# Normed rows written by VectorE into the PSUM banks of the expert sums

## The chip, the cores and the metric

The kernel runs on one core of one Trainium2 chip. The metric is the device time of one execution in microseconds. Everything is float32.

## The reference

Two transformer blocks over 256 tokens of width 1024 run one after the other. What matters here is the first block, which has two layers. Each layer is a mixer (a convolution module in layer 0, a differential attention in layer 1), a layer norm, a mixture of experts, and a second layer norm:

```
for l in range(DEPTH):
    mix = conformer_conv(...) if l < N_A else diff_attention(...)
    x = layer_norm(ALPHA * x + mix, ln_mix_g[l], ln_mix_b[l])
    ffn = grouped_moe(x, router_w, router_bias, moe_w_gate[l], moe_w_up[l], moe_w_down[l])
    x = layer_norm(ALPHA * x + ffn, ln_ffn_g[l], ln_ffn_b[l])
```

`layer_norm` is `(x - mean) * rsqrt(var + 1e-5) * g + b` over the 1024 columns. `grouped_moe` picks two of 16 experts for each token by a sigmoid router, and adds `(silu(x @ wg) * (x @ wu)) @ wd` of the chosen experts with weights that sum to one. The sum over the experts is added to `ALPHA * x`, so the normed rows x are both the input of the experts and a term of their sum.

## The kernel before

**Stages.** One program writes a queue for each engine (TensorE as `pe`, ScalarE as `act`, VectorE as `dve`, GpSimd as `pool`, SyncE as `sp`), stage after stage in the list `ORDER`. Most stages have no barrier between them; engines meet through semaphores. Tokens are two tiles of 128 rows, t = 1 and 2. PSUM has 8 banks of 128 x 512. Banks 0 to 3 are taken in turn by numbered jobs: `take_bank(j)` waits until the bank was read out, `job_done` counts finished jobs, and `job_ready(eng, j)` lets an engine wait for job j. Banks 4 to 7 hold running sums: `layer_sum(t)` is the pair of banks 4, 5 for t = 1 and 6, 7 for t = 2.

**Around the change, layer 0.** In `conformer`, banks 4 to 6 hold the sums for a norm over the channels. Then `project_and_turn` multiplies the activated convolution output with `pw2`: four parts of eight 128x512 products (L623), each part a 512-column half of a tile; the first part waits chunk by chunk for ScalarE's SiLU (`act_ready`, L1033). VectorE adds the residual, takes mean and variance and writes the normalized, unscaled rows to `xhat[t - 1]` (L602, `centred_scaled`). TensorE transposes them (L531) and ScalarE and VectorE copy the transposes out with gain and bias to `xT` (L556, L558). Only then does VectorE run `natural_rows`: for each tile xhat times gain into `x_nat` (L610), then `x_nat` plus bias into `x_nat` (L611). `natural_rows` is called three times: by `mix_norm` (k = 0), by `ffn_norm` of layer 0 (k = 1) and by `mix_norm1` (k = 2).

**The router** (`route`, once for each layer). TensorE multiplies `xT` with the router's weights (L1211), ScalarE copies the parts (L1152), TensorE sums them (L1217), ScalarE takes the sigmoid (L1154). VectorE, behind `natural_rows` in its queue, ranks the experts in some 17 small dependent operations (L1167 to L1193), and the last of them raises `won_ready`. Meanwhile TensorE puts x into the sums as products of x with the identity (L1224), two halves for each tile, with `start=True`, so that the experts' products, all with `start=False`, add to it. Behind them in TensorE's queue stand jobs J + 2 and J + 3 (L255, narrow products that count each expert's tokens), which wait for `won_ready`. VectorE turns job J + 2 into seats (L1202, then L1427). ScalarE copies `x_nat` in another order of columns to `by_row` (L1158), once for each tile, and raises `rows_ready`.

**The experts** (`experts`). TensorE waits for `rows_ready` and for the seats and gathers the tokens of the first pair of experts (`gather`, L255, 32 records of 128x128), then multiplies with the gate and up weights of each expert (L1565), transposes, multiplies with the down weights (L1598) and scatters into banks 4 to 7 (L1608). The expert weights, 48 units of 2 MB for each layer, are streamed by SyncE's queue (L421) in order. Each unit waits until the last product on the slot that it overwrites: in each layer the unit issued after pair 0's first gate and up products (`GU0`) is the first of the pair's slots to come free. Two of the extra slots lie in `x_nat` and `norm_rows`; they wait for `rows_ready` and for job J + 2.

Of the kernel before, what the change touches and what calls it, by code (L numbers as in the profile page):

```python
# [25 lines left out]
ALU = mybir.AluOpType  # L26
# [5 lines left out]
KC = D // P  # L32
# [30 lines left out]
BANKS = 4  # L63
# [47 lines left out]
def first_jobs():  # L111
    at, out = 0, {}
    for name, n in JOBS:
        out[name] = at
        at += n
    return out
# [41 lines left out]
def program(nc, a, out):  # L158
# [3 lines left out]
    def sb(name, *shape):  # L162
        return ctx.enter_context(nc.sbuf_tensor(name, list(shape), F32))

    def sem(name):
        return ctx.enter_context(nc.semaphore(name))

    FJ = first_jobs()
# [5 lines left out]
    x_nat = sb("x_nat", P, 3, D)  # L174
    xT = sb("xT", P, KC, L)
    norm_rows = sb("norm_rows", P, 2, 2, D)
    vec = sb("vec", P, len(VEC_ROWS) * P)
    ident = sb("ident", P, P)
    ones = sb("ones", P, P)
# [22 lines left out]
    psum = ctx.enter_context(nc.psum_tensor("psum", [P, 8, 512], F32))  # L202
# [14 lines left out]
    dve_step, act_step = Chain(nc.vector, sem("dve_step")), Chain(nc.scalar, sem("act_step"))  # L217
# [18 lines left out]
    def bank(j):  # L236
        return psum[:, j % BANKS, :]

    def take_bank(j):

        if j >= BANKS:
            nc.tensor.wait_ge(bank_free[j % BANKS], j // BANKS)

    def job_ready(eng, j):
        eng.wait_ge(job_done, j + 1)
# [6 lines left out]
    def products(dst, pairs):  # L252

        for n, (lhsT, rhs) in enumerate(pairs):
            last = nc.tensor.matmul(dst, lhsT, rhs, start=(n == 0), stop=(n == len(pairs) - 1))  # L255
        return last
# [15 lines left out]
    unit_at = {}  # L272
# [83 lines left out]
    def slot(u):  # L356
        return arena[:, 6690:6690 + 4096] if slots[u] == RING else ring[:, slots[u], :]
# [8 lines left out]
    def slot_k(u, n=512):  # L366

        return slot(u).rearrange("p (k n) -> p k n", n=n)

    def unit_ready(u):  # L370
        nc.tensor.wait_ge(slot_loaded[slots[u]], landed[u])
# [214 lines left out]
    xhat = carve(13300, D), carve(5664, D)  # L586
# [11 lines left out]
    def centred_scaled(t, root, normed, src, dst):  # L598
# [2 lines left out]
        reciprocal_of(nc.vector, var, root)  # L601
        nc.vector.tensor_scalar(dst, src, mean, var, ALU.subtract, ALU.mult).then_inc(normed, 1)  # L602

    def natural_rows(k, normed, xhat=xhat):

        dve = nc.vector
        dve.wait_ge(norm_loaded[k % 2], 32 * (k // 2 + 1))
        dve.wait_ge(normed, 2)
        for t in (1, 2):
            dve_step(dve.tensor_tensor(x_nat[:, t, :], xhat[t - 1], norm_rows[:, k % 2, 0, :], ALU.mult))  # L610
            dve.tensor_tensor(x_nat[:, t, :], x_nat[:, t, :], norm_rows[:, k % 2, 1, :], ALU.add).then_inc(normed, 1)  # L611

    def project_and_turn(first, u0, lhs, normed, ready=None):

        pe = nc.tensor

        def part(j, half, t):
            unit_ready(u0 + half)
            take_bank(j)
            for k in range(KC):  # L620
                if ready is not None and half == 0:
                    ready(k, t)
                last = pe.matmul(bank(j), lhs(k, t), slot_k(u0 + half)[:, k, :], start=(k == 0), stop=(k == KC - 1))  # L623
            last.then_inc(job_done, 1)

        def turn(j, t):
            transposes_pe(j, (t,), lambda t: xhat[t - 1], lambda t: pe.wait_ge(normed, t))

        part(first, 0, 1)
        part(first + 1, 1, 1)  # L630
        part(first + 2, 0, 2)
        turn(first + 3, 1)
        part(first + 5, 1, 2)
        turn(first + 6, 2)
# [237 lines left out]
    mean_summed, conv_normed, act_ready = sem("mean_summed"), sem("conv_normed"), sem("conv_activated")  # L872
    normed = [sem(f"normed{k}") for k in range(4)]
# [3 lines left out]
    def conformer():  # L877
# [3 lines left out]
        def _(pe):  # L881
# [67 lines left out]
            for c in (6, 7):  # L949
# [5 lines left out]
            products(bank(FJ["iota"])[:, 0:P], [(ones[:, :], upto[:, :])]).then_inc(job_done, 1)  # L955
            take_bank(FJ["relb"])
            products(bank(FJ["relb"])[0:HEADS, 0:3 * P], [(rel_w[:, :], buckets)]).then_inc(job_done, 1)
            project_and_turn(FJ["mix0"], unit_at["pw2"], lambda k, t: conv[:, k, (t - 1) * P:t * P], normed[0],
                             ready=lambda k, t: pe.wait_ge(act_ready, KC * (t - 1) + k + 1))

# [162 lines left out]
    by_row = carve(4640, 2, KC, P)  # L1123
# [11 lines left out]
    def layer_sum(t):  # L1135

        return psum[:, BANKS + 2 * t - 2:BANKS + 2 * t, :].rearrange("p b n -> p (b n)")
# [7 lines left out]
    def route(layer):  # L1145
# [3 lines left out]
        @block.scalar  # L1149
        def _(act):  # L1150
            job_ready(act, J)
            act.activation(parts, bank(J)[:, 0:SEQ], ACT.Copy).then_inc(bank_free[J % BANKS], 1)  # L1152
            job_ready(act, J + 1)
            act.activation(aff[:, :, :], bank(J + 1)[:, 0:2 * EXPERTS].rearrange("p (t e) -> p t e", t=2),  # L1154
                           ACT.Sigmoid).then_inc(aff_ready, 1)
            for t in range(2):
                act.wait_ge(normed[2 * layer], 3 + t)
                act_step(act.activation(by_row[:, t, :, :], x_nat[:, t + 1, :].rearrange("p (f k) -> p k f", k=KC),  # L1158
                                        ACT.Copy))
            act.nop().then_inc(rows_ready, 1)  # L1160

# [44 lines left out]
        @block.tensor  # L1206
        def _(pe):
            all_read_out(pe, J)
            for r in range(2):
                for g in range(CONV_GROUPS):  # L1210
                    last = pe.matmul(bank(J)[32 * g:32 * g + 32, 0:SEQ], router_w[:, 4 * r + g, :],  # L1211
                                     xT[:, 4 * r + g, META:L], start=(r == 0), stop=(r == 1))
            last.then_inc(job_done, 1)
            take_bank(J + 1)
            pe.wait_ge(bank_free[J % BANKS], J // BANKS + 1)
            for t in range(2):
                last = pe.matmul(bank(J + 1)[:, t * EXPERTS:t * EXPERTS + EXPERTS], parts[:, t * P:t * P + P],  # L1217
                                 quad_diag[:, 0:EXPERTS], start=True, stop=True)
            last.then_inc(job_done, 1)

            for t in (1, 2):
                pe.wait_ge(normed[2 * layer], 2 + t)
                for half in range(2):
                    pe.matmul(psum[:, BANKS + 2 * t - 2 + half, :], ident[:, :], x_nat[:, t, half * 512:half * 512 + 512],  # L1224
                              start=True, stop=False, skip_group_check=True)
            take_bank(J + 2)
            take_bank(J + 3)
            pe.wait_ge(won_ready, layer + 1)
            n = EXPERTS
            products(bank(J + 2)[:, 0:n], [(upto[:, :], beats[:, 0, :])])  # L1230
            products(bank(J + 2)[:, n:2 * n], [(ones[:, :], beats[:, 0, :]), (upto[:, :], beats[:, 1, :])]).then_inc(
                job_done, 1)
            products(bank(J + 3)[:, 0:n], [(ones[:, :], beats[:, 0, :]), (ones[:, :], beats[:, 1, :])]).then_inc(job_done, 1)
# [1819 lines left out]
```

## Time and profile before

| | |
|---|---|
| median of 3 runs | 1397.87 us (1395.96 to 1400.76) |
| the profiled execution's own time | 1401.46 us |
| its span | 1399.7 us |
| TensorE matmul busy | 1306.0 us, 93% |
| VectorE busy | 383.9 us, 27% |
| ScalarE busy | 262.6 us, 19% |
| bytes moved | 321.68 MB, mean 230 GB/s |
| chain that ended last | PE 87%, DMA 5%, DVE 5% |

### The profile page before, as it was taken

Reading aid. Unit: us, or ns where it says so; the run is one execution under the profiler, and the core shown is the slowest. Engines: PE = TensorE matmul, PEld = TensorE weight load, DVE = VectorE, ACT = ScalarE, POOL = GpSimd, SP = SyncE. Lnnn points to the kernel's source line nnn. Section 1 sums busy time; section 2 is a strip of 40 time slices with the busy share of each in tenths; the row PEclk is TensorE's granted clock in tenths of the full one; section 3 lists DMA queues with packets and bytes.
Section 4 is the critical chain, followed back from the end, with each engine's and each line's share of the span. In section 5 each row is a group of like instructions: output and inputs, shape, how many; then the busy total and the mean of one; then the engine's idle time right before and its main releaser. Section 6 shows DMA issues by size and latency. Waiting matters only on the chain.

```text
span 1399.7 us, 14987 instructions
## 1 busy us (share of the span) xinstructions
PE 1306.0 (93%) x6166; PEld 815.9 (58%) x6166; DVE 383.9 (27%) x849; ACT 262.6 (19%) x579; POOL 36.0 (3%) x62
## 2 busy tenths in 40 slices
PE   7989899999989998999999799998998979999997
PEld 6754444333437864433433388765775867888743
DVE  0014522111142454312211403455223123222101
ACT  1013311000111343200100321412435012000000
POOL 3110000000000000000000000000000000000000
PEclk9999999999999998999999899899999998999999
DMA  9970899999992063999999923231230162444320
GB/s 307 309 249 2 324 407 428 425 423 429 415 380 86 1 240 147 418 426 424 427 427 427 393 109 121 67 110 43 84 120 1 35 193 73 153 147 161 141 90 30
DMA packets 95087, 321.68 MB, mean 230 GB/s; under 512 B 10099, under 2 KB 47511, under 8 KB 80167
## 3 DMA queue, kind: packets, MB, share of 16 engines
q1 hardware_dynamic: 84368, 301.04, 55.5%
q10 hardware_dynamic: 8662, 12.27, 2.8%
q0 software_dynamic: 1984, 7.34, 1.3%
q8 instruction: 53, 0.87, 0.3%
q14 instruction: 20, 0.16, 0.0%
HBM read 316.30 MB, written 4.34 MB: 229 GB/s over the span
## 4 chain that ended last, share of the span: by engine, by line
PE 87%; DMA 5%; DVE 5%; issue 1%; ACT 1%; DVEq 0%; ACTq 0%; SPq 0%; POOLq 0%
PE psum L255 35%; PE psum L1565 14%; PE psum L1598 7%; PE psum L741 6%; PE psum L2917 5%; DMA ring<-in_moe_w_up 5%; PE psum L1608 4%; PE psum L623 2%; PE psum L909 2%; PE psum L1802 2%; PE psum L531 1%; PE psum L1767 1%; DMA ring<-in_a_w_pw 1%; PE psum L2577 1%; PE psum L1224 1%
## 5 line engine op out<-in xcount | busy, mean ns | idle before, releaser
L255 PE MATMUL psum<-xT,ring 128*128 128x256 f32 (+2 forms) x1792 | 409.7, 390 | 4.6 <-DMA ring<-in_a_w_pw 3.7
L255 PEld LDWEIGHTS psum<-xT,ring 128*128 128x128 f32 x1792 | 344.9, 194 | 65.4 <-issue 10.4
L1565 PE MATMUL psum<-ring,arena 128*64 128x512 f32 x672 | 186.0, 604 | 12.1 <-DMA ring<-in_moe_w_up 6.6
L1565 PEld LDWEIGHTS psum<-ring,arena 128*64 128x64 f32 x672 | 59.8, 139 | 103.1 <-issue 102.8
L1446 DVE TENSOR_TENSOR arena<-psum,arena 64x512 f32<-64x512 f32 x32 | 34.2, 1070 | 215.7 <-ACT arena L1509 215.7
L1598 PE MATMUL psum<-ring,arena 128*64 128x512 f32 x384 | 85.0, 595 | 1.3 <-ACT arena L1526 1.3
L2917 PE MATMUL psum<-ring,arena 128*128 128x512 f32 x176 | 75.7, 592 | 0.0
L1565 PE MATMUL psum<-arena 128*64 128x512 f32 x208 | 70.6, 592 | 0.0
L1509 ACT ACTIVATE arena<-psum 64x512 f32<-64x512 f32 x32 | 18.9, 592 | 269.8 <-PE psum L1565 269.8
L1608 PE MATMUL psum<-arena 128*128 128x512 f32 x128 | 59.5, 605 | 0.0
L2917 PEld LDWEIGHTS psum<-ring,arena 128*128 128x128 f32 x176 | 33.4, 190 | 41.7 <-issue 41.6
L1598 PEld LDWEIGHTS psum<-ring,arena 128*64 128x64 f32 x384 | 27.4, 137 | 51.7 <-issue 51.5
L741 PE MATMUL psum<-arena,ring 128*128 128x258 f32 x256 | 55.8, 381 | 0.0
L255 PE MATMUL psum<-arena 128*128 128x128 f32 (+3 forms) x372 | 52.8, 291 | 1.9 <-issue 1.9
L741 PEld LDWEIGHTS psum<-arena,ring 128*128 128x128 f32 x256 | 48.6, 190 | 7.0
L255 PEld LDWEIGHTS psum<-arena 128*128 128x128 f32 (+1 forms) x372 | 43.5, 182 | 10.0 <-issue 9.2
L531 PE MATMUL psum<-ident,arena 128*128 128x128 f32 (+1 forms) x120 | 19.3, 324 | 29.6 <-DVE arena L2069 19.1
L1608 PEld LDWEIGHTS psum<-arena 128*128 128x128 f32 x128 | 22.8, 189 | 35.0 <-issue 35.0
L1470 DVE COPY arena<-psum 128x512 f32<-128x512 f32 x16 | 11.1, 692 | 98.7 <-PE psum L1598 98.7
L531 PEld LDWEIGHTS psum<-ident,arena 128*128 128x128 f32 (+1 forms) x120 | 16.9, 180 | 34.4 <-DVE arena L2069 20.2
L2944 ACT ACTIVATE arena<-arena 128x256 f32<-128x256 f32 x22 | 9.2, 416 | 143.1 <-DVE arena L2961 143.1
L909 PE MATMUL psum<-arena 128*32 128x256 f32 x512 | 31.0, 396 | 4.7 <-issue 4.7
(343 smaller groups left out, 1310.2 us busy)
## 6 DMA issues: line engine op xcount, KB each, us to landing
ring<-in_moe_w_down SPq DMA_DIRECT2D x24, 2048.0 KB, 24.9
ring<-in_moe_w_up SPq DMA_DIRECT2D x22, 2048.0 KB, 20.7
ring<-in_moe_w_gate SPq DMA_DIRECT2D x20, 2048.0 KB, 22.7
ring<-in_w_in SPq DMA_DIRECT2D x11, 2048.0 KB, 22.3
ring<-in_w_up SPq DMA_DIRECT2D x22, 1024.0 KB, 7.7
arena<-in_moe_w_gate SPq DMA_DIRECT2D x6, 2048.0 KB, 26.3
ring<-in_w_down SPq DMA_DIRECT2D x5, 2048.0 KB, 7.8
ring<-in_a_w_pw SPq DMA_DIRECT2D x8, 1024.0 KB, 10.9
```

The lines of the kernel that those rows point to most:

```text
L255: last = nc.tensor.matmul(dst, lhsT, rhs, start=(n == 0), stop=(n == len(pairs) - 1))
L531: last = nc.tensor.transpose(bank(j)[:, c * P:c * P + n], src(t)[0:n, at:at + P], ident[0:n, 0:n])
L623: last = pe.matmul(bank(j), lhs(k, t), slot_k(u0 + half)[:, k, :], start=(k == 0), stop=(k == KC - 1))
L741: last = nc.tensor.matmul(bank(first + c)[:, NEED:L], slot_k(part_units[half])[:, k, (c % 4) * P:(c % 4) * P + P], src[:, k, NEED:L], star ...
L909: last = pe.matmul(bank(j)[32 * g:32 * g + 32, 0:SEQ], blocks[:, c % BLOCK_BUFS, q, g, :], shifted[:, c % REP_BUFS, g, 4 * q:4 * q + SEQ], ...
L1446: dve.tensor_tensor(hid_both[part, :].rearrange("s (k f) -> s k f", f=P), by_row(bank(j)[part, :]), by_row(silu_g[part, 0, :]), ALU.mult). ...
L1509: act.activation(silu_g[UP_IN[side], 0, :], bank(j)[GATE_IN[side], :], ACT.Silu).then_inc(silu_ready, 1)
L1565: last = pe.matmul(bank(j)[part, :], tokens[:, k, side * SEATS:side * SEATS + SEATS], weights(u + n, k), start=(k == 0), stop=(k == KC - 1))
L1598: last = pe.matmul(bank(j)[part, :], hidT_both[:, k, side * SEATS:side * SEATS + SEATS], weights(u + side, k, D)[:, half * 512:half * 512 ...
L1608: last = pe.matmul(psum[:, BANKS + 2 * t + half, :], gatedT[:, p % 4, t * P:t * P + P], y_pair[:, half * 512:half * 512 + 512], start=Fals ...
L1802: last = pe.matmul(psum[:, BANKS + 2 * (t - 1) + half, :], oT[:, h, TILE_AT[t]:TILE_AT[t] + P], slot_k(unit_at["w_o"] + half)[:, h, :], st ...
L2917: last = pe.matmul(psum[:, BANKS + 2 * t + half, :], fT[:, c, t * P:t * P + P], slot_k(u, D)[:, c % 4, half * 512:half * 512 + 512], start ...
```

## The change

In `natural_rows` the second operation of each tile writes into `layer_sum(t)`, the two PSUM banks, where k is even; for k = 1 it still writes `x_nat`. The first operation works in place in `xhat`, so VectorE first waits for the job that transposed that tile (`turned_job`). ScalarE's copy to `by_row` reads `layer_sum` in place of `x_nat`. The four products with the identity are gone in both layers. PSUM keeps a flag for each element that says whether a product adds or overwrites, and only products set it; so in layer 0, ahead of `project_and_turn`, four products of one row are put in, one for each of banks 4 to 7, whose result is later overwritten. They wait for the weights of `pw2` and for the first SiLU.

```diff
+    def turned_job(k, t):
+
+        return FJ["mix0"] + (4, 7)[t - 1] if k == 0 else FJ["ffn0_xT" if k == 1 else "mix1"] + 2 * t - 1
+
     def natural_rows(k, normed, xhat=xhat):
 
         dve = nc.vector
         dve.wait_ge(norm_loaded[k % 2], 32 * (k // 2 + 1))
         dve.wait_ge(normed, 2)
         for t in (1, 2):
-            dve_step(dve.tensor_tensor(x_nat[:, t, :], xhat[t - 1], norm_rows[:, k % 2, 0, :], ALU.mult))
-            dve.tensor_tensor(x_nat[:, t, :], x_nat[:, t, :], norm_rows[:, k % 2, 1, :], ALU.add).then_inc(normed, 1)
+            job_ready(dve, turned_job(k, t))
+            dst = x_nat[:, t, :] if k % 2 else layer_sum(t)
+            dve_step(dve.tensor_tensor(xhat[t - 1], xhat[t - 1], norm_rows[:, k % 2, 0, :], ALU.mult))
+            dve.tensor_tensor(dst, xhat[t - 1], norm_rows[:, k % 2, 1, :], ALU.add).then_inc(normed, 1)
...
+            unit_ready(unit_at["pw2"])
+            pe.wait_ge(act_ready, 1)
+            for b in range(BANKS, 2 * BANKS):
+                pe.matmul(psum[:, b, :], ones[0:1, :], slot_k(unit_at["pw2"])[0:1, 0, :], start=True, stop=True)
             project_and_turn(FJ["mix0"], unit_at["pw2"], lambda k, t: conv[:, k, (t - 1) * P:t * P], normed[0],
...
-                act_step(act.activation(by_row[:, t, :, :], x_nat[:, t + 1, :].rearrange("p (f k) -> p k f", k=KC),
+                act_step(act.activation(by_row[:, t, :, :], layer_sum(t + 1).rearrange("p (f k) -> p k f", k=KC),
                                         ACT.Copy))
...
-            for t in (1, 2):
-                pe.wait_ge(normed[2 * layer], 2 + t)
-                for half in range(2):
-                    pe.matmul(psum[:, BANKS + 2 * t - 2 + half, :], ident[:, :], x_nat[:, t, half * 512:half * 512 + 512],
-                              start=True, stop=False, skip_group_check=True)
```

## Rows read from the trace of the kernel before

**Rows 1.** Chain that ended last, layer 0: start us, us, what.

```profile
119.06 23.78 PE psum L623 x48
160.00 4.85 PE psum L1224 x8
```

**Rows 2.** Timeline before and in the `pw2` projection: start us, us, engine, line.

```profile
115.66 0.81 PE L255 MATMUL psum<-arena,rel_w 32*8 32x384 f32 x2
118.42 3.86 ACT L1033 ACTIVATE arena<-arena,vec 128x128 f32<-128x128 f32 x8
120.90 0.34 PEld L623 LDWEIGHTS psum<-ring,arena 128*128 128x128 f32 x1 [0.52 <-issue]
121.75 0.34 PEld L623 LDWEIGHTS psum<-ring,arena 128*128 128x128 f32 x1 [0.52 <-ACT arena L1033]
137.53 5.31 PE L623 MATMUL psum<-ring,arena 128*128 128x512 f32 x12
```

**Rows 3.** Timeline of the router, layer 0.

```profile
158.99 1.01 PE L1217 MATMUL psum<-quad_diag,arena 128*128 128x16 f32 x4 [0.59 <-ACT arena L1152]
159.77 1.23 DVE L611 TENSOR_TENSOR x_nat<-x_nat,norm_rows 128x1024 f32<-128x1024 f32 x1
159.84 5.01 PE L1224 MATMUL psum<-x_nat,ident 128*128 128x512 f32 x8
160.04 0.20 ACT L1154 ACTIVATE arena<-psum 128x32 f32<-128x32 f32 x1 [1.19 <-PE psum L1217]
160.13 4.16 ACT L1158 ACTIVATE arena<-x_nat 128x1024 f32<-128x1024 f32 x2
164.30 0.19 DVE L1193 SCALAR_TENSOR_TENSOR arena<-arena 128x32 f32<-128x32 f32 x1
164.69 0.31 PE L255 MATMUL psum<-arena,upto 128*128 128x16 f32 x2
165.56 0.19 DVE L1202 TENSOR_TENSOR arena<-arena,psum 128x32 f32<-128x32 f32 x1 [0.19 <-PE psum L255]
166.84 3.81 PE L255 MATMUL psum<-arena 128*128 128x128 f32 x32 [0.94 <-issue]
```

**Rows 4.** Timeline of the router, layer 1.

```profile
557.66 5.77 PE L1224 MATMUL psum<-x_nat,ident 128*128 128x512 f32 x8
562.13 0.19 DVE L1193 SCALAR_TENSOR_TENSOR arena<-arena 128x32 f32<-128x32 f32 x1
563.28 0.29 PE L255 MATMUL psum<-arena,upto 128*128 128x16 f32 x2
```

**Rows 5.** Group of instructions by line: count, then busy us and mean ns.

```profile
L602 DVE TENSOR_SCALAR arena<-psum,small 128x1024 f32<-128x1024 f32 x4 | 5.4, 1344 | 0.1
```

**Rows 6.** Stretches: from:to us, length, PE busy (records), PEclk, DMA share, GB/s.

```profile
124.00:125.00 1.00, 1.00 (x2) 0.51 0.00 0
155.00:156.00 1.00, 0.00 (x0) 0.85 1.03 442
162.00:163.00 1.00, 1.00 (x3) 0.73 0.84 352
343.00:344.00 1.00, 1.00 (x6) 0.78 1.04 442
882.00:883.00 1.00, 1.00 (x10) 0.87 1.08 414
```

**Rows 7.** Timeline of TensorE at a wait for weights and at narrow products.

```profile
340.44 5.98 PE L1565 MATMUL psum<-ring,arena 128*64 128x512 f32 x20 [2.69 <-DMA ring<-in_moe_w_up]
879.19 4.75 PE L255 MATMUL psum<-w_dt,xT 128*16 128x16 f32 x48
```

**Rows 8.** Timeline of SyncE's queue, layer 0.

```profile
177.71 0.33 SPq L421 DMA_DIRECT2D ring<-in_moe_w_up  x1
```

**Rows 9.** Stretches: from:to us, length, PEclk, DMA share, GB/s.

```profile
178.00:180.00 2.00, 1.00 0.81 193
578.50:579.00 0.50, 1.00 1.06 377
```

## The prediction

> **What bounds the kernel now.** I read the chain of waits first. It runs through TensorE for 87% of the span, and both places that the change touches lie on it: the `pw2` projection as one unbroken piece of 23.78 us, and the identity products with 4.85 us in layer 0 [rows 1]. A piece on the chain is only what its engine did while the next thing was awaited, so I then read the timeline around each to see what else ended at the same moment.
>
> In layer 0's router the identity products are issued at 159.84 and job J + 2 behind them starts at 164.69. VectorE's last ranking operation ends at 164.30 + 0.19 = 164.49, and a start 0.20 us behind it is what the semaphore alone would give. So VectorE's chain and the identity products end together, and taking the products away frees nothing there [rows 3]. In layer 1 VectorE ends at 562.32 and J + 2 starts at 563.28; with the same 0.20 us it could start at 562.52, so the products hold it up by about 0.75 us [rows 4]. Behind that come the seats, which ride on J + 2 (read by VectorE at 165.56), and then the gather at 166.84. ScalarE's copies to `by_row` end at 164.29, 2.5 us before the gather needs them [rows 3].
>
> VectorE's chain itself starts where `natural_rows` ends, at 161.00, not at the sigmoid, which ended at 160.24 [rows 3]. So the two writes into PSUM are on the path.
>
> Then the views by stretches, for TensorE's clock and the DMA. The clock is at its lower level (1.2 GHz, 0.50) from about 155.7 to 162.5 us: TensorE had been mostly idle ahead of 155.7, and it rose again while the identity products ran [rows 3, 6]. It is full when the gather starts. The DMA runs at some 426 GB/s through most of each expert stage. The PE waits 2.69 us for weights late in layer 0's stage [rows 7], so the end of the stage is set by the queue of weight transfers, and that by the last place where the queue ran dry. In layer 0 this is at 178 to 180 us, where it moved 193 GB/s; the unit that fills it again is issued at 177.71, on the heels of pair 0's first products [rows 8, 9]. In layer 1 the same place shows a mere dent, 377 GB/s for half a microsecond [rows 9]: 0.06 us lost. So whatever makes pair 0 later makes the stage later in layer 0 one for one, and in layer 1 too after a margin that I take as 0.2 us; making it earlier gains at most the hole, (1 - 193/426) x 2 = 1.1 us in layer 0, and nothing in layer 1.
>
> **The change part by part.**
>
> *Four products of one row, added.* Each is two records. A record of 512 columns takes 5.31/12 = 0.43 us at the full clock, and 0.85 us at the lower one (starts at 120.90 and 121.75) [rows 2]. That the operand has one row should not shorten it: two records of 384 columns with 32 rows took 0.81 us [rows 2], no less than their columns ask for. They wait for the first SiLU, as the projection does. The SiLUs come at 3.86/8 = 0.48 us [rows 2] and the projection needs two records for each, so TensorE, not ScalarE, sets the pace from 119.06 on, and nothing hides the four. The clock was low from there to about 124.98, 5.9 us after the products began [rows 1, 6]. If the added products count as work for the clock like the ones that they displace, the low stretch holds them in place of the projection's first records, which then run at the full clock: the cost is 8 x 0.43 = 3.4 us. If they don't, it is 8 x 0.85 = 6.8 us. I take 3.4, since streaming columns is what the displaced ones do too. This delays everything behind, the weight transfers also: those of layer 0 wait for the projection's jobs.
>
> The Trainium skill, "PSUM — Partial Sum Buffer", under "The four PSUM rules", says that VectorE's writes leave the add-or-overwrite bits alone, and that a seed other than zero should go in through TensorE by an identity product. That speaks against this change and is the reason for the added products; without it the sum would be 3.4 us smaller. No row of this trace shows the bits.
>
> *`natural_rows`.* The same four operations. The multiplies stay as they are. No row shows VectorE writing PSUM. Nearest is one reading PSUM, 1.344 us for 128x1024 [rows 5], against 1.23 for the add into SBUF [rows 3]: between 0 and 0.12 us more for each of two tiles. I take 0.06, so 0.1 us on each layer's path. The added waits are for transposes that `scaled_out` in the same queue has already waited for: nothing. For k = 1 VectorE works beside TensorE's attention projections: nothing.
>
> *The copy to `by_row` from PSUM.* 4.16/2 = 2.08 us now; it would have to take over 3.3 us each (2.08 + 2.5/2) to matter, and it may be faster, which gains nothing since the seats come last [rows 3]. Zero.
>
> *The identity products, gone.* 0 in layer 0 and -0.75 in layer 1, from above. But they were also what TensorE did while it waited. Without them it is idle from the end of L1217 at 160.0 until J + 2 at about 164.6, and the clock, low at 160, has nothing to bring it back. J + 2 and J + 3 are too narrow for that: 48 records of 16 columns kept TensorE "busy" for 4.75 us, and the clock fell at the end of them [rows 6, 7]. So J + 2 starts at the lower level. L1217 there shows 0.25 us for such a record, against some 0.14 for the six of J + 2 now (164.69 to about 165.5): 6 x 0.1, with less for the weight load's share, makes 0.5 us [rows 3].
>
> The gather is then the first dense work. How long does the low clock last behind such a start? After 119.06 it was 5.9 us; after 340.44 about 3.0 [rows 1, 6, 7]. I take the middle, 4.5 us. Gather and first expert products are paced by TensorE at half speed in it, so half is lost: 2.25 us, from 1.5 to 3.0. I choose this over no loss because the clock was already low when the idle stretch began.
>
> The Trainium skill, "TensorE: Matmul & The Clock Gate", under "The HAM clock gate", has it that the lower clock is the default and activity releases it. By that rule the gather pays; by a clock that came back by itself it would not, and the sum would be 4.5 us smaller. The rows agree with the rule.
>
> *The sum.* Layer 0: 3.4 + 0.1 + 0.5 + 2.25 = 6.25 us, all of it passed on by the dry weight queue. Layer 1: 0.1 + 0.5 + 2.25 - 0.75 - 0.2 = 1.9. Together 8.15 us on the profiled execution's own 1401.46, so 1409.6. That execution was 3.6 us above the median of the runs shown; on 1397.87 the same sum gives 1406.0, which I take.
>
> **The rivals.**
>
> *The clock is back for the gather.* If the small products or the neighbouring work bring it back, 3.4 + 0.1 + 0.5 remain in layer 0 and nothing in layer 1: 4.0 us, 1401.9. For it: layer 0's low stretch was over 2.7 us into the identity products [rows 3, 6]. Against it: 2.5 us of that came behind continuous dense work that is gone.
>
> *The added products don't count for the clock.* Then 3.4 more: 1409.4. Nothing in the trace has so few rows.
>
> *The weight queue hides the gather.* If queued transfers reach further than I read, the slower start of pair 0 is absorbed by the PE's later wait of 2.69 us, and 3.5 to 4 us remain: 1401.6. The hole at 178 us speaks against it [rows 9].
>
> *The identity products were the bound (the other side).* If the chain is taken at its word, 4.85 us go in layer 0 and about as much in layer 1 (5.77 us busy), less 3.4 added: about -7 us, 1391. It decides only if VectorE's ranking would end that much sooner, or the copies to `by_row` were what the gather waited for and became quick from PSUM. VectorE's own end at 164.49 speaks against it [rows 3].
>
> **How the numbers follow.** About 0.3% (4.2 us) is what a measurement of this kernel tells from no change. The forecast gets 0.50, with its own range of 1402.5 to 1409.5 (loss at the gather 1.5 to 3.0 in each layer, PSUM writes 0 to 0.25, and the spread of the runs). The clock rival has 0.22, the uncounted products 0.12, the queue 0.08, the other side 0.08. Slower by over 0.3%: nearly all of the forecast and of the uncounted products, and a third of the two at 1401.6 to 1401.9, so 0.70. Faster 0.08, the rest 0.22. For 8 in 10 the range reaches from the two cases near 1401.7, less the spread of the runs, to the uncounted products: 1398 to 1411.
>
> **What would show it.** L623 unbroken as before, behind eight records of one row that take about 5.9 us at the low clock, with the projection's end 3.4 us later against its first SiLU. `natural_rows` at about 1.22 and 1.23 to 1.35 us. An idle TensorE between L1217 and J + 2, PEclk 0.50 through J + 2 and into the gather, and the gather at about 6 to 7 us in place of 3.81. The unit issued behind pair 0's first products later against the start of the gather, and a deeper hole in the DMA behind it, in layer 1 a first one. The prediction is wrong if the gather still takes 3.8 us, if the added products take the place of idle time, or if layer 1's expert stage ends no later against its attention.

## The result, and the profile after

The changed kernel takes 1405.03 us (median of 6 runs, 1404.13 to 1410.46), the kernel before 1398.51 beside it (6 runs, 1395.96 to 1400.76). The ratio is 1.0056, with an interval of 1.0035 to 1.0076: 7.8 us slower, between 4.9 and 10.6. The prediction was 1406.0, or 8.15 us slower than the 1397.87 that it started from. The profiled execution of the changed kernel took 1404.13 us, its span 1402.4, against 1401.46 and 1399.7 before. These two single executions are only 2.7 us apart: the one of after is the fastest of its six. So the runs carry the size of the effect, and the profiles its place.

The engines' busy time, from the head of the page of after:

```profile
span 1402.4 us, 14972 instructions
PE 1302.7 (93%) x6158; PEld 818.7 (58%) x6158; DVE 384.0 (27%) x849; ACT 258.3 (18%) x579; POOL 35.9 (3%) x62
```

TensorE's time fell by 3.3 us and ScalarE's by 4.3, and the kernel became slower. The totals cannot tell why, so I read the two places in their order. First the projection, in TensorE's timeline of after (start us, us, engine, line, out<-in, count, and in brackets the idle time before it and what ended it):

```profile
112.41 0.81 PE L255 MATMUL psum<-arena,rel_w 32*8 32x384 f32 x2
115.81 5.56 PE L967 MATMUL psum<-ring,ones 1*128 1x512 f32 x8 [2.59 <-ACT arena L1043]
121.30 9.87 PE L629 MATMUL psum<-ring,arena 128*128 128x512 f32 x19
```

and in its stretches (from:to us, length, PE busy and records, PEclk, DMA share, GB/s); the last three belong to the router and to layer 1:

```profile
117.00:118.00 1.00, 1.00 (x3) 0.72 0.00 0
120.00:121.00 1.00, 1.00 (x2) 0.50 0.00 0
124.00:125.00 1.00, 1.00 (x3) 0.87 0.00 0
161.00:165.00 4.00, 0.22 (x2) 0.50 0.97 412
168.00:172.00 4.00, 3.46 (x16) 0.50 1.00 405
580.00:583.00 3.00, 3.00 (x16) 1.00 0.87 251
```

The eight records of one row sit in front of the projection and take 5.56 us, the first at the full clock and the rest at the lower one. The clock falls while they run and is back at about 124.3, some 3 us into the projection. In before, no product ran between the same idle time of 2.59 us and the projection, and the projection itself paid for the low clock [rows 2, 6].

The router of layer 0 in after, from its timeline:

```profile
160.22 1.00 PE L1227 MATMUL psum<-quad_diag,arena 128*128 128x16 f32 x4 [0.58 <-ACT arena L1162]
161.00 1.23 DVE L617 TENSOR_TENSOR psum<-arena,norm_rows 128x1024 f32<-128x1024 f32 x1
161.35 2.07 ACT L1168 ACTIVATE arena<-psum 128x1024 f32<-128x1024 f32 x2
165.52 0.19 DVE L1203 SCALAR_TENSOR_TENSOR arena<-arena 128x32 f32<-128x32 f32 x1
165.86 0.58 PE L255 MATMUL psum<-arena,upto 128*128 128x16 f32 x2 [4.64 <-DVE arena L1203]
167.40 0.19 DVE L1212 TENSOR_TENSOR arena<-arena,psum 128x32 f32<-128x32 f32 x1 [0.81 <-PE psum L255]
168.68 5.41 PE L255 MATMUL psum<-arena 128*128 128x128 f32 x32 [0.54 <-issue]
```

This answers to [rows 3]. TensorE is idle for 4.64 us where the identity products stood, the clock is 0.50 through that wait, and the gather takes 5.41 us where it took 3.81. The write into PSUM takes 1.23 us, as the write into SBUF did. The copy to `by_row` takes 1.03 us for each tile where it took 2.08. The unit behind pair 0 is issued at 181.16, in before at 177.71 [rows 8]; in the ten microseconds from 178 the transfers move 238 GB/s, and in before in the ten from 176 they moved 365.

Layer 1, in the same view:

```profile
564.24 0.19 DVE L1203 SCALAR_TENSOR_TENSOR arena<-arena 128x32 f32<-128x32 f32 x1
564.58 0.58 PE L255 MATMUL psum<-arena,upto 128*128 128x16 f32 x2 [5.51 <-DVE arena L1203]
567.41 5.71 PE L255 MATMUL psum<-arena 128*128 128x128 f32 x32 [0.54 <-issue]
```

Job J + 2 now follows VectorE at 0.15 us, where it stood 0.96 us behind it [rows 4], and runs at half speed, as does the gather. From 580 to 583 us there is a hole in the weight transfers, 251 GB/s, that before did not have [rows 9].

**How executions are compared below.** Two executions of one kernel differ by several microseconds in places that an edit does not touch: the first SiLU starts at 118.42 in before and at 115.17 in after, with nothing changed ahead of it. So I measure intervals between points of the same execution. For the rest of the document they are, in us (all of them differences of two starts in a timeline):

- A, projection: start of the first SiLU to the start of VectorE's last residual addition, which waits for the projection's last part
- B, router of layer 0: from there to the gather
- C, the gather of layer 0, to the first expert product
- D, from the end of A to the issue of the weights behind pair 0
- E, from the end of A to the end of layer 0's expert sum (where `ffn_norm` starts to write normed rows)
- F, G, H: for layer 1, from the issue of the weights that waits for the attention's output product, to the weights behind pair 0 (F) and to the end of the expert sum (G); H is the gather

| | A | B | C | D | E | H | F | G |
|---|---|---|---|---|---|---|---|---|
| before | 32.20 | 16.22 | 3.74 | 27.09 | 243.23 | 3.74 | 30.10 | 246.73 |
| after | 36.23 | 17.28 | 5.35 | 29.76 | 244.97 | 5.64 | 31.48 | 246.78 |
| e1 | 39.05 | 17.76 | 3.74 | 28.62 | 244.10 | 3.74 | 31.41 | 248.16 |
| e2 | 30.89 | 17.36 | 3.74 | 28.23 | 244.61 | 5.27 | 31.63 | 246.99 |
| e3 | 36.23 | 16.52 | 3.74 | 27.39 | 242.69 | 5.16 | 31.20 | 246.69 |
| e4 | 33.60 | 16.84 | 6.00 | 29.97 | 246.10 | 5.32 | 31.62 | 246.99 |
| e5 | 30.06 | 16.83 | 5.92 | 29.88 | 245.99 | 5.25 | 31.62 | 247.13 |
| e6 | 30.06 | 16.91 | 3.74 | 27.78 | 244.21 | 3.74 | 29.46 | 246.00 |
| e7 | 29.26 | 17.41 | 3.74 | 28.28 | 244.83 | 3.74 | 30.10 | 246.41 |
| e8 | 39.04 | 16.83 | 6.15 | 30.11 | 246.34 | 8.76 | 35.06 | 250.48 |
| e9 | 29.26 | 17.01 | 3.74 | 27.88 | 243.32 | 3.74 | 29.51 | 245.61 |
| e10 | 29.25 | 17.69 | 3.74 | 28.56 | 243.91 | 3.74 | 31.46 | 246.70 |

(In e8, H holds four added products. Each row is one execution.)

### The profile page after: what moved, and what is told of

The parts are those of the page before. It is cut to its first block, busy times and chain, and to the rows that moved or that the text cites. A ratio compares the mean times of both kernels' runs of the same rounds, so it can differ in the third digit from the quotient of the medians.

```text
span 1402.4 us, 14972 instructions
## 1 busy us (share of the span) xinstructions
PE 1302.7 (93%) x6158; PEld 818.7 (58%) x6158; DVE 384.0 (27%) x849; ACT 258.3 (18%) x579; POOL 35.9 (3%) x62
## 4 chain that ended last, share of the span: by engine, by line
PE 81%; DMA 10%; DVE 6%; ACT 1%; issue 1%; ACTq 0%; DVEq 0%; SPq 0%; POOLq 0%
PE psum L255 35%; PE psum L1570 12%; PE psum L1603 6%; PE psum L747 6%; PE psum L2922 5%; DMA ring<-in_moe_w_up 4%; DMA arena<-in_moe_w_up 4%; PE psum L1613 3%; PE psum L629 2%; PE psum L1807 2%; PE psum L915 1%; PE psum L531 1%; PE psum L1772 1%; DMA glu_scratch<-arena 1%; DMA ring<-in_a_w_pw 1%
## 5 line engine op out<-in xcount | busy, mean ns | idle before, releaser
L1570 PE MATMUL psum<-arena 128*64 128x512 f32 x208 | 74.0, 610 | 0.0
L255 PE MATMUL psum<-arena 128*128 128x128 f32 (+3 forms) x372 | 56.3, 304 | 1.1 <-issue 1.1
L255 PEld LDWEIGHTS psum<-arena 128*128 128x128 f32 (+1 forms) x372 | 47.0, 195 | 9.2 <-issue 8.4
```

The lines of the kernel that those rows point to most:

```text
L1570: last = pe.matmul(bank(j)[part, :], tokens[:, k, side * SEATS:side * SEATS + SEATS], weights(u + n, k), start=(k == 0), stop=(k == KC - 1))
```

## The experiments

Ratios are against the kernel before, beside runs of it, with their intervals. Its medians there were 1398.26 for e1 to e4, 1398.34 for e5 to e8, and 1398.0 for e9 and e10. None of these kernels changes what is computed; the added products go into banks that are overwritten later.

### e1: only the four products

The kernel before, with the added products and nothing else of the change.

```diff
+            unit_ready(unit_at["pw2"])
+            pe.wait_ge(act_ready, 1)
+            for b in range(BANKS, 2 * BANKS):
+                pe.matmul(psum[:, b, :], ones[0:1, :], slot_k(unit_at["pw2"])[0:1, 0, :], start=True, stop=True)
             project_and_turn(FJ["mix0"], unit_at["pw2"], ...
```

> The kernel before, with the four one-row products in front of the pw2 projection and nothing else of the change. My theory: they have no cover and stand on the path, so the projection ends 3.4 to 4.0 us later against its first SiLU, and the time is 3.4 to 4.0 us above before (1402 on 1398.5). The rival that the removal of the identity products and the writes into PSUM cost most: then this kernel is within 1 us of before.

Measured: 1403.76 us (12 runs), ratio 1.0034 (1.0019 to 1.0048), so 4.8 us slower, between 2.7 and 6.7. The timeline of TensorE in e1, and a stretch of it:

```profile
116.47 7.16 PE L961 MATMUL psum<-ring,ones 1*128 1x512 f32 x8 [2.59 <-ACT arena L1037]
123.56 7.66 PE L623 MATMUL psum<-ring,arena 128*128 128x512 f32 x11
```

```profile
128.00:129.00 1.00, 1.00 (x3) 0.51 0.00 0
```

The eight records take 7.16 us, all at the low clock, and the clock is still low at 129, 5.4 us after the first product with 128 rows. In before the low stretch was 5.9 us from the first such product on [rows 1, 6]. The added products hardly shortened it. Over half of the change's cost is here: 4.8 of 7.8 us. It is more than the 3.4 to 4.0 that was expected, and the rival of "within 1 us of before" is out.

### e2: the change in layer 1 only

Layer 0 as in the kernel before, the four products left out; the identity products of layer 0, each with `start=True`, set the flags that layer 1 needs.

```diff
+            dst = layer_sum(t) if k == 2 else x_nat[:, t, :]
...
+                src = layer_sum(t + 1) if layer else x_nat[:, t + 1, :]
...
-            for t in (1, 2):
+            for t in (1, 2) if layer == 0 else ():
```

> The kernel before, with the change made in layer 1 alone (rows into PSUM, copy from PSUM, no identity products there); layer 0 as it was, so no one-row products. My theory as predicted: +1.9 us, from the gather at half clock less the 0.75 us that the identity products held up. The rival that the weight queue and the waits for it absorb a late pair 0 gives 0 (1398.5), with the gather still slow (5 to 6 us in place of 3.8). The rival that the identity products were the bound gives -2 to -5 us.

Measured: 1399.24 us (12 runs), ratio 1.0006 (0.9992 to 1.002): 0.8 us, between -1.1 and 2.8: told apart neither from nothing nor from the 1.9 that was predicted. The gather of layer 1 is slow all the same (H 5.27), and the weights behind pair 0 come 1.5 us later than in before's profile (F 31.63), yet the stage ends where it did (G 246.99). What is lost in front of layer 1's experts does not reach the end in this trace.

### e3: the clock kept in the router

The changed kernel with three products ahead of the wait for `won_ready`, in both layers: the identity with weights that have landed, into a bank of job J + 3.

```diff
             take_bank(J + 3)
+            unit_ready(unit_at[f"moe{layer}"])
+            for n in range(3):
+                pe.matmul(bank(J + 3), ident[:, :], slot_k(unit_at[f"moe{layer}"])[:, n, :], start=True, stop=True)
```

> The changed kernel, with three products of the identity with landed weights into a bank that is overwritten later, in the place in TensorE's queue where the identity products stood; they wait for nothing of VectorE. Nothing of them is used. Theory: the clock comes back in them or soon after, jobs J + 2 and J + 3 and the gather run at full rate or nearly, gather 3.8 to 4.5 us, and layer 0's expert stage ends 1.5 to 2.5 us sooner against its projection; in all 1402 to 1404. Rival, that the gather is slow for another reason (reads from by_row, seats): gather still 5.4 us and the time that of the changed kernel, 1405, or more.

Measured: 1403.11 us (9 runs), ratio 1.0041 (1.0024 to 1.0058); the changed kernel's is 1.0056. TensorE's timeline of e3, around the gather of layer 0 and of layer 1, and a stretch ahead of the second:

```profile
161.81 5.14 PE L1235 MATMUL psum<-ring,ident 128*128 128x512 f32 x6
168.92 3.81 PE L255 MATMUL psum<-arena 128*128 128x128 f32 x32 [0.94 <-issue]
566.29 5.23 PE L255 MATMUL psum<-arena 128*128 128x128 f32 x32 [0.95 <-issue]
```

```profile
565.00:566.00 1.00, 0.34 (x4) 0.93 1.01 356
```

In layer 0 the gather is back at 3.81 us, D is 2.4 us and E 2.3 us shorter than in after. So the slow gather is the clock, and it is passed on there. In layer 1 the clock came back under the three products and fell again through the end of the narrow products and the wait behind them; the gather stayed slow. The gain in the runs, 1.5 points in a thousand or 2 us, is as expected, but the two intervals overlap: the traces carry this finding, not the times.

### e4: the four products in idle time

In the changed kernel the four products are released as soon as the banks are free and no longer wait for the first SiLU. Before that, TensorE stood idle for 2.59 us.

```diff
             unit_ready(unit_at["pw2"])
-            pe.wait_ge(act_ready, 1)
-            for b in range(BANKS, 2 * BANKS):
+            for b in (BANKS, 2 * BANKS - 1, BANKS + 1, BANKS + 2):
+                if b == BANKS + 1:
+                    pe.wait_ge(var_ready, 1)
                 pe.matmul(psum[:, b, :], ones[0:1, :], slot_k(unit_at["pw2"])[0:1, 0, :], start=True, stop=True)
```

> The changed kernel, with the four one-row products released earlier: two of them by nothing, the two whose banks VectorE still reads by the semaphore of its last read of them, in place of the first SiLU. They then fall in the idle 2.6 us in front of the projection. Theory: one microsecond of the four is left on the path, and the clock does not fall in front of the projection (that cost about 3 us of half rate), so the projection ends 5 to 6 us sooner against its first SiLU and the time is 1399 to 1400.5. Rival, that the clock falls all the same because one-row products do not count for it: 2.5 us less than the changed kernel, 1402.5.

Measured: 1402.16 us (12 runs), ratio 1.0028 (1.0016 to 1.0041); A is 33.60 where after had 36.23. TensorE's timeline and stretches:

```profile
117.01 0.81 PE L255 MATMUL psum<-arena,rel_w 32*8 32x384 f32 x2
117.75 4.66 PE L968 MATMUL psum<-ring,ones 1*128 1x512 f32 x8
122.34 9.09 PE L629 MATMUL psum<-ring,arena 128*128 128x512 f32 x15
```

```profile
119.00:120.00 1.00, 1.00 (x4) 1.00 0.00 0
120.00:121.00 1.00, 1.00 (x3) 0.67 0.02 8
126.00:127.00 1.00, 1.00 (x3) 0.50 0.00 0
```

TensorE is busy without a gap from 117.01 on. Still the clock falls at about 120.3, while the one-row products run, and is low until about 127.2. The 1399 to 1400.5 us that were expected did not come; the rival, 1402.5 because one-row products do not count for the clock, is what was measured.

### e5: the same place, 128 rows in place of one

e4, and the products now have 128 rows. The same banks, the same columns, the same number of records.

```diff
-                pe.matmul(psum[:, b, :], ones[0:1, :], slot_k(unit_at["pw2"])[0:1, 0, :], start=True, stop=True)
+                pe.matmul(psum[:, b, :], ident[:, :], slot_k(unit_at["pw2"])[:, 0, :], start=True, stop=True)
```

> The kernel of e4 with one thing changed: the four products that set the flags have all 128 rows (the identity times 128 rows of landed weights) in place of one row; same number, same columns, same place, result overwritten as before. Theory, that one-row products do not count as work for the clock: now it does not fall in front of the projection, the projection ends 29 to 31 us after the first SiLU in place of 33.6, and the time is 2.5 to 4 us less than e4's 1402.2, so 1398 to 1399.5. Rival, that the clock falls there whatever the products are (a share of idle time, the 64-column products before them): no change from e4.

Measured: 1399.77 us (12 runs), ratio 1.0007 (0.9993 to 1.0021), 2.4 us below e4 by the medians, with intervals that overlap a little. TensorE's timeline and stretches of e5:

```profile
111.81 0.81 PE L255 MATMUL psum<-arena,rel_w 32*8 32x384 f32 x2
112.55 3.70 PE L968 MATMUL psum<-ring,ident 128*128 128x512 f32 x8
116.08 15.18 PE L629 MATMUL psum<-ring,arena 128*128 128x512 f32 x35
```

```profile
115.00:116.00 1.00, 1.00 (x3) 1.00 0.00 0
118.00:119.00 1.00, 1.00 (x3) 1.00 0.00 0
```

The clock never falls, eight records take 3.70 us, and A is 30.06, less than before's 32.20. The two kernels differ in the number of rows, and with it in the values (the identity in place of ones), and in nothing else: the one-row products do not count for the clock. The traces are one execution each, but the runs agree: the granted clock over the whole span, mean of 12 runs, is 0.962 in e4 and 0.964 in e5, and a low stretch of 6.9 us (120.3 to 127.2) at half clock is 3.4/1404 = 0.0024 of the span. e5's A is still 0.8 us longer than that of e7 below, which sets no flags. e9 moves two of the four products elsewhere and has e7's 29.26, so the flags of four banks can be had for nothing in layer 0.

### e6: all three repairs of the clock

e5 and e3 together, and one more such product between job J + 3 and the gather, ahead of the wait for `rows_ready`.

```diff
+            free(gathers(0)[1])
+            unit_ready(U)
+            pe.matmul(bank(gathers(0)[1]), ident[:, :], slot_k(U)[:, 0, :], start=True, stop=True)
             pe.wait_ge(rows_ready, layer + 1)
```

> e5 and e3 together, and one more product of the identity with landed weights (into a bank that the gather overwrites) between jobs J + 2, J + 3 and the gather in both layers. Theory: the gains of e5 (about 6 us against the changed kernel) and of e3 (2 us) add, and the gather is full speed in layer 1 too: 1396 to 1398. Rival, that layer 1's repair is absorbed like its loss and the extra product delays the gather by up to 0.9 us: 1397 to 1399.

Measured: 1394.95 us (12 runs), ratio 0.9977 (0.9961 to 0.9992): 3.2 us below before, by the ratios 11 below the changed kernel, and a little less than the 1396 to 1398 that were expected. In layer 1, TensorE's timeline:

```profile
560.74 0.40 PE L255 MATMUL psum<-arena,upto 128*128 128x16 f32 x2
561.88 1.10 PE L1632 MATMUL psum<-ring,ident 128*128 128x512 f32 x2
562.98 3.81 PE L255 MATMUL psum<-arena 128*128 128x128 f32 x32
```

Both gathers run at 3.74 to the first expert product, and F is 29.46, the shortest so far. The way to the gather is 18.59 us (G's start to the gather) where before took 19.23, and e2, e4 and e5, at the low clock, 19.18 to 19.24: 0.64 us less, near the 0.75 that was predicted for the identity products of layer 1. (In after it was 18.71 even so.)

### e7: the kernel before, with the clock kept

Is e6's gain over before the change's own, or the repairs'? The kernel before, with three unused products of 128 rows in the idle time ahead of the projection and nothing else.

```diff
+            unit_ready(unit_at["pw2"])
+            for n in range(3):
+                pe.matmul(psum[:, 2 * BANKS - 1, :], ident[:, :], slot_k(unit_at["pw2"])[:, n, :], start=True, stop=True)
             project_and_turn(FJ["mix0"], unit_at["pw2"], ...
```

> The kernel before, with three products of the identity with landed weights put in the idle 2.6 us in front of the projection; nothing else changed, nothing of them used. It shows what the clock alone was worth there. Theory: the clock does not fall, the projection ends 28.5 to 30 us after the first SiLU in place of 31 to 32, so 1396 to 1397. If it is the four products' own time that counts and not the clock, no change or +0.5 us.

Measured: 1393.89 us (12 runs), ratio 0.9974 (0.9955 to 0.9994). Three idle-time products give before all that e6 had. It is 2 us less than the 1396 to 1397 expected. The gain is the projection's clock: A is 29.26, 2.9 us less than before's and 1.6 less than e2's, and the granted clock over the span, mean of 12 runs, is 0.968 against 0.966 in the runs of before beside them.

### e8: pair 0 later in layer 1

The changed kernel with four more products ahead of pair 0's first expert product, in layer 1 only. This asks how much delay layer 1 absorbs before it passes it on.

```diff
+                if p == 0 and layer == 1:
+                    free(job("GU0", 0))
+                    unit_ready(U)
+                    for n in range(4):
+                        pe.matmul(bank(job("GU0", 0)), ident[:, :], slot_k(U)[:, n, :], start=True, stop=True)
                 read_out(pe, gathers(p)[0])
```

> The changed kernel, with four more products of the identity with landed weights in front of pair 0's first gate and up products in layer 1 alone: 3.4 us at the full clock, up to 6.9 if it is still low. It measures how much of a late pair 0 reaches the end of the stage. Theory of the prediction, that the weight queue passes it on one for one: +3.4 to 4 us on 1405.0. The rival that e2 points to, that the waits for weights late in the stage absorb it: +0 to 1.5 us.

Measured: 1409.34 us (6 runs), ratio 1.0086 (1.0062 to 1.011), 4.3 us above the changed kernel. TensorE's and SyncE's lines of e8:

```profile
577.35 3.60 PE L1634 MATMUL psum<-ring,ident 128*128 128x512 f32 x8
588.01 0.33 SPq L421 DMA_DIRECT2D ring<-in_moe_w_up  x1
```

F grows by 3.4 to 3.6 us over the four executions with the change in layer 1 and no repair there (31.48 to 31.63), and G by 3.5 over their mean. So past the delay that the change itself brings, layer 1 passes on one for one, as the theory had it.

### e9 and e10: the last idle stretch ahead of the projection

Both put two products of 128 rows into an idle stretch further ahead, behind the sum over the shifts: e9 in e6 (two of its four products are moved there), e10 in e7 (two unused ones are added). The lines of e10:

```diff
             shift_sum()
+            unit_ready(unit_at["pw2"])
+            for n in range(2):
+                pe.matmul(psum[:, 2 * BANKS - 1, :], ident[:, :], slot_k(unit_at["pw2"])[:, n, :], start=True, stop=True)
```

> e6 with two of the four flag-setting products (banks 7 and 4) moved some 24 us further ahead, into the idle stretch in front of the sixth chunk's taps (about 2.5 to 3.5 us in the traces), so that two remain in front of the projection. Theory: the projection ends 28.4 to 29 us after the first SiLU in place of 30.0, so 1 to 1.5 us less than e6's 1394.95: 1393.5 to 1394. Rival, that the two delay the taps, whose inputs come by DMA at varying times: no gain, 1395 to 1396.

> e7 (the kernel before with three unused products in front of the projection) with two more unused products in the idle stretch in front of the sixth chunk's taps. It is the equal of e9 without the change. Theory: the clock seldom falls in front of those taps either, which spares 0 to 1 us: 1393 to 1394, the same as e9 within 1 us, so that the change is worth nothing once the clock is kept. If the change has a value of its own, e9 is 1.5 us or more below this one.

Measured: e9 1394.0 us (12 runs), ratio 0.9976 (0.996 to 0.9993); e10 1393.05 us (12 runs), ratio 0.9966 (0.995 to 0.9982). The interval of each holds the other's ratio, and e7's: the second stretch is worth 1 us by the ratios, within the intervals, and the change with every repair shows no gain over the kernel before with its clock kept. The fastest of all kernels is e10, which has nothing of the change in it, 4.8 us below before. TensorE's timeline of e10:

```profile
91.97 1.88 PE L942 MATMUL psum<-ring,ident 128*128 128x512 f32 x4
112.31 2.84 PE L963 MATMUL psum<-ring,ident 128*128 128x512 f32 x6
114.99 17.39 PE L623 MATMUL psum<-ring,arena 128*128 128x512 f32 x40
```

## Why the prediction was right, and where its terms were not

The forecast case held: slower, by 8.15 us predicted and 7.8 measured, through the places that it named. One term was too small and those of the two routers too large, so that the total says more for the prediction than its steps deserve. The four products cost 1.4 to 2.7 us more than forecast, layer 0's router 1.1 less and layer 1 1.9 less. That these nearly cancelled is luck. One of the prediction's own signs of being wrong did come: layer 1's expert stage ended no later against its attention (G 246.78 after, 246.73 before).

**The four products, predicted 3.4 us, measured 4.8 to 6.1.** This is the term that was mis-sized. The step was "I take 3.4, since streaming columns is what the displaced ones do too", and it was wrong: the rival of the uncounted products, at 6.8, described what happens. The low stretch ran through the added records and then on through the projection, for 3.0, 3.4, 5.4 and 5.4 us of it (after, e3, e1, e8), where without them it was 5.9 and 3.3 (before, e2). So the added products did nothing to bring the clock back. A in the four executions with one-row products in place (after, e1, e3, e8) is 36.23, 39.05, 36.23 and 39.04, mean 37.6; with none (before, e2) 32.20 and 30.89, mean 31.5: 6.1 us. The runs of e1 give 4.8 (2.7 to 6.7). It is less than 6.8 in part because some of the records still run at the full clock when the fall comes late, as the first ones of after and e3 do (both 36.23; in e1 and e8, where all eight are slow, A is 39.05 and 39.04). The proof is e4 against e5: same place, same columns, no gap, and the clock falls with one row and not with 128. Whether it is the rows or the values was not separated. The Trainium skill, "TensorE: Matmul & The Clock Gate", under "The HAM clock gate", says that activity releases the clock; the traces agree with that and show that being busy in the timeline is not the same thing.

**The writes into PSUM, predicted 0.1 us a layer, measured 0.** L617 takes 1.23 us, L611 took 1.23 [rows 3].

**The copy from PSUM.** It may be faster and gains nothing, the prediction said: 1.03 us for 2.08. It ends at 163.42 in after, 5 us ahead of the gather, so nothing waited for it; no run tests it alone.

**The identity products of layer 0, predicted to free nothing.** B without them is 16.8 to 17.3 (after, e4, e5, e8: mean 16.95), with them 16.22, 17.76, 17.36, 17.41 and 17.69 (before, e1, e2, e7, e10: mean 17.29). The profile that I read was the odd one, in which they ended with VectorE's chain and job J + 2 started 0.20 us behind it. In e1, e2, e7 and e10 J + 2 started 1.77, 1.10, 1.43 and 1.70 us behind VectorE; without the identity products it was 0.15. So taking them away more than paid for the slower J + 2: B fell by 0.34 us, where the sum had it 0.6 longer.

**The gather at the low clock, predicted 2.25 us in each layer, measured 2.1 and 1.6.** C is 5.35, 6.00, 5.92 and 6.15 without the identity products, mean 5.86, and 3.74 in every execution with them. In layer 1, H is 5.64, 5.27, 5.32 and 5.25, mean 5.37. e3 gives the cause: with the clock kept, C is 3.74.

**Passed on in layer 0, one for one.** D is longer by 29.93 - 28.16 = 1.77 us, E by 245.85 - 244.14 = 1.71, means of the same four and five. The prediction had 2.85 for D without the projection's part. The step held; the amount was smaller mostly because of B.

**Layer 1, predicted 1.9 us, measured nothing in the traces.** F is longer by 31.59 - 30.77 = 0.8 us (after, e2, e4, e5 against before, e1, e7, e10), and G by 246.97 - 247.00 = 0.0. The second figure leans on e1, whose 248.16 is far from its fellows; without it G is 0.4 longer. e2's 0.8 us, with its wide interval, agrees with either. Two steps were at fault. The first is the delay of pair 0 itself, predicted as 2.1 us (1.9 and the margin of 0.2): the gather lost 1.6 and not 2.25, and the identity products held J + 2 up by more than in the trace that was read, J + 2 starting 0.96, 1.80, 0.91 and 1.86 us behind VectorE (before, e1, e7, e10). The second is the margin of 0.2 us, which was read from a dent of 0.06 us in the transfers: the stage took up most of F's 0.8 us. e8 shows that a further delay is passed on in full. What takes the first one up is not shown. Since the hole of 580 to 583 us costs the queue (1 - 251/426) x 3 = 1.2 us, something later must be shorter. The chain that ended last, in before and then in after, shows a candidate (start us, us, what):

```profile
739.26 8.78 PE psum L1565 x32
```

```profile
713.45 8.80 PE psum L1570 x32
...
772.47 7.09 PE psum L1570 x32
```

The block of 32 records behind a wait for weights takes 8.8 us when the clock has fallen in the wait, and 7.1 when not. In after (and in e2 to e5 and e8 alike) the slow block comes one wait earlier and the last one is at the full clock. But e10, with layer 1 as in before, has the pattern of after as well, so this is not the change's own doing. It is still the likely place: e1 and e10 have the same layer 1 and nearly the same F (31.41 and 31.46), e1 has the pattern of before and a G of 248.16, e10 that of after and 246.70, 1.5 us less. These are two executions; no run tests it, and what decides the pattern stays open.

**The sum as measured.** 6.1 + 1.7 + 0.0 = 7.8 us, against 7.8 (4.9 to 10.6) in the runs. With e1's 4.8 for the first term it is 6.5. Each term has the spread of a few executions, over a microsecond for A, so the sum fits, and its closing to the tenth means nothing.

**The rivals.** The clock back for the gather: false, C and H. The added products that don't count for the clock: true as a mechanism, while its total of 1409.4 came out too high because the routers cost less. The weight queue hides the gather: false in layer 0 (E), true in layer 1 for the little that the change delays it there. The identity products as the bound: false as to 7 us; they did hold J + 2 up by a microsecond or more in most executions, but with every cost of the change repaired e6 and e9 are no faster than e7 and e10. The Trainium skill, "PSUM — Partial Sum Buffer", under "The four PSUM rules", advises to put in a seed other than zero by an identity product; here that advice is right in time as well, since the seed by VectorE showed no gain even where its flags cost nothing (e9 against e10). The change without its four products was not tried, so that the flags need them is not shown by a run.

## What to carry to other kernels

Work on TensorE that waits in the shadow of another engine is not free to take away, when it is also what keeps the clock up: look at what runs next, and at which clock. Judge a warm-up or a flag-setting product by its place and its shape: in idle time and with 128 rows, e5's four cost nothing and even gained, ahead of the first awaited product and with one row they cost 5 to 6 us. And before an edit is costed from one trace, see whether the two things that end together there do so in other executions too.

## What the runs showed of the hardware

- Products of one row and 512 columns, back to back, did not keep the granted clock up (e4: 1.00 at 119 to 120, 0.67 at 120 to 121, low to 127.2) nor bring it back (e1: low through 7.16 us of them and 5.4 us beyond). The same products with 128 rows kept it at 1.00 (e5). A one-row record takes no less time than a full one: 7.16/8 = 0.90 us at the low clock (e1), against 0.85 from start to start for full ones [rows 2].
- Narrow products did not hold it either: in before the clock fell at about 882.7 us in the midst of 48 records of 16 columns that kept TensorE busy without a gap from 879.19 on [rows 6, 7]. In layer 1 of e3 it fell in the 2.6 us of such records and of waits between the three added products and the gather (0.93 from 565 to 566 us), and the gather at 566.29 took 5.23 us; in layer 0 of e3 the same stretch was 2.0 us long and the gather took 3.81. With one 128x512 product right ahead of the gather it took 3.81 in layer 1 as well (e6).
- ScalarE's copy of 128x1024 in another order of columns takes 1.03 us when it reads PSUM and 2.08 when it reads SBUF.
- VectorE's 128x1024 add takes 1.23 us whether it writes SBUF or PSUM.
- Three products that nobody uses, in a gap of 2.59 us, made the kernel before 3.6 us faster (e7, 0.8 to 6.3), and five in two gaps 4.8 us (e10, 2.5 to 7.0).
